# The head of a one-core encoder layer, rearranged: values before queries and keys, the norm factors applied elsewhere

## The reference, cut to what matters

```python
h = x * rsqrt(mean(x*x, axis=-1) + 1e-6) * norm_mix        # x: (512, 1024), one factor per token, one per channel
P = h @ w_in                                               # columns [q_A k_A v_A q_B k_B v_B u_C gates]
q, k = rms_norm(q_A, g_q), rms_norm(k_A, g_k)              # per head of 64
A = softmax(q k^T / 8 + bias) v_A                          # branch A; B: stick-breaking attention; C: pooling
y = (sig(g_A)*(A W_a) + sig(g_B)*(B W_b) + sig(g_C)*(C W_c)) @ W_out
x = x + y
x = x + W_down( silu(conv(hg)) * conv(hv) )                # [hg|hv] = rms_norm(x) @ W_up
```

## Time and profile before

| | us |
|---|---|
| median of 3 runs | 835.34 (834.24 to 835.59) |
| the profiled execution | 834.84 |
| its span in the trace | 832.7 |
| TensorE busy in the span | 815.1 (98%), 3855 matmuls |
| DVE, ACT, GpSimd busy | 601.5, 402.6, 102.1 |

### The profile page before, as it was taken

One profiled execution on the slowest core, in us unless ns is written; L12 is line 12 of the kernel. 1 busy time (PEld: TensorE's weight loads), 2 busy tenths in 40 slices (PEclk: granted clock), 3 DMA queues, 4 the chain that ended last, 5 costly groups with the idle time before them and its releaser, 6 DMA issues.

```text
span 832.7 us, 11778 instructions
## 1 busy us (share of the span) xinstructions
PE 815.1 (98%) x3855; PEld 677.1 (81%) x3855; DVE 601.5 (72%) x847; ACT 402.6 (48%) x560; POOL 102.1 (12%) x87
## 2 busy tenths in 40 slices
PE   5999999999999999999999999999999999899998
PEld 4888888888888888888888887888888888688886
DVE  5535888867678676555552579888778789998798
ACT  6434776665546544434341463433333334455653
POOL 2100010000000060000000013332232333300000
PEclk9999999999999999999999999999999999999999
DMA  6333242222222222333363326666556655666455
GB/s 207 103 102 89 66 124 77 79 74 66 86 76 66 74 77 88 93 98 100 89 214 104 129 72 202 203 202 201 189 191 199 196 191 185 218 210 191 149 186 177
DMA packets 129964, 113.25 MB, mean 136 GB/s; under 512 B 6052, under 2 KB 109192, under 8 KB 128528
## 3 DMA queue, kind: packets, MB, share of 16 engines
q1 hardware_dynamic: 129264, 110.77, 42.6%
q0 software_dynamic: 672, 2.12, 0.9%
HBM read 99.21 MB, written 13.65 MB: 136 GB/s over the span
## 4 chain that ended last, share of the span: by engine, by line
PE 93%; DVE 4%; ACT 1%; DMA 1%; issue 1%; SPq 0%; DVEq 0%; ACTq 0%
PE ps L1422 29%; PE ps L1423 28%; PE ps L1424 28%; PE ps L1516 2%; PE ps L1506 2%; PE ps L1531 1%; PE ps L1530 1%; DVE w_lo L872 1%; DMA x_in<-in_x_dram 1%; DVE conv_out L1259 1%; DVE out_sb L1412 0%; DVE conv_out L1262 0%; PE ps L1447 0%; DVE conv_in L1268 0%; ACT w_hi L497 0%
## 5 line engine op out<-in xcount | busy, mean ns | idle before, releaser
L1422 PE MATMUL ps<-h_lo,w_hi 128*128 128x512 f32 x704 | 276.9, 393 | 1.5 <-DVE h_lo L897 0.9
L1423 PE MATMUL ps<-h_hi,w_hi 128*128 128x512 f32 x704 | 274.2, 389 | 0.0
L1424 PE MATMUL ps<-h_hi,w_lo 128*128 128x512 f32 x704 | 274.1, 389 | 0.0
L872 DVE TENSOR_TENSOR w_lo<-w_raw,w_hi 128x1024 fp32r<-128x1024 f32 x119 | 149.8, 1259 | 137.3 <-ACT w_hi L503 77.9
L503 ACT ACTIVATE w_hi<-w_raw 128x1024 fp32r<-128x1024 f32 x97 | 102.8, 1060 | 191.9 <-PE ps L1424 183.4
L1422 PEld LDWEIGHTS ps<-h_lo,w_hi 128*128 128x128 f32 x704 | 132.2, 188 | 29.8 <-issue 1.6
L1424 PEld LDWEIGHTS ps<-h_hi,w_lo 128*128 128x128 f32 x704 | 132.2, 188 | 27.6
L1423 PEld LDWEIGHTS ps<-h_hi,w_hi 128*128 128x128 f32 x704 | 132.2, 188 | 26.5
L481 POOL TENSOR_TENSOR sg<-sg,conv_out 128x512 f32<-128x512 f32 x22 | 37.4, 1700 | 319.2 <-ACT sg L801 319.2
L1262 DVE SCALAR_TENSOR_TENSOR conv_out<-conv_in,par,conv_out 128x512 f32<-128x512 f32 x44 | 50.2, 1141 | 5.5 <-DVE conv_out L1259 0.2
L497 ACT ACTIVATE w_hi<-w_raw 128x1024 fp32r<-128x1024 f32 x23 | 24.4, 1059 | 53.3 <-PE ps L1424 53.2
(11 more groups left out here) (219 smaller groups left out, 1304.7 us busy)
## 6 DMA issues: line engine op xcount, KB each, us to landing
w_raw<-in_w_in_dram SPq DMA_DIRECT2D x104, 256.0 KB, 3.1
w_raw<-in_w_up_dram SPq DMA_DIRECT2D x88, 256.0 KB, 3.2
raw_t<-in_w_down_dram SPq DMA_DIRECT2D x11, 1024.0 KB, 9.1
down_sums<-t_sum SPq DMA_DIRECT2D x11, 1024.0 KB, 5.6
w_raw<-in_w_down_dram SPq DMA_DIRECT2D x33, 256.0 KB, 3.0
w_raw<-down_sums SPq DMA_DIRECT2D x33, 256.0 KB, 3.8
w_raw<-in_w_out_dram SPq DMA_DIRECT2D x16, 256.0 KB, 2.9
w_raw<-down_sums SPq DMA_DIRECT2D x22, 128.0 KB, 2.9
```

What stands on the lines that cost most here:

```text
L872: v.tensor_tensor(w_lo[:, slot, :], w_raw[:, slot, :], r32(w_hi[:, slot, :]), ALU.subtract)\
L1422: mm3(dst, l_hi, r_lo, start=start, stop=False, **kw)
L1423: mm3(dst, l_hi, r_hi, start=False, stop=False, **kw)
L1424: return mm3(dst, l_lo, r_hi, start=False, stop=stop, **kw)
```

## The change

The same mathematics, put differently. For the values v = diag(r) * x * diag(g) * W, with r the factor per token and g the norm weight per channel: now x itself is turned as it lands and split (`xt_hi`, `xt_lo`), g is multiplied into the weight rows when a unit of v is split (`values_hi`, `values_lo`), and r is applied when v is copied out of PSUM. So the values need no norm factors to begin. The order of units on PE becomes: v_A in units 0 to 3, the first unit of v_B (unit 4), q and k (units 5 and 6), and the rest of v_B (units 7 to 9). For q and k, and all later tiles, h is still made: the two parts of turned x are added on DVE (`h_sum`), r is spread over the partitions by two matmuls of a diagonal (`d_r_hi`, `d_r_lo`, bank `R_BANK`), and h_sum * g * r is split into `h_hi` and `h_lo`. All of that stands on ACT and DVE between the splits of the value units. The squares of x are summed later, with the first value units. At the very start PE gets 24 matmuls of 128 columns on constants, whose result is not used. The load of `g_row` moves to ACT's queue. GpSimd's one weight split is gone. `sumsq` for q and k stands after unit 7, and `newton` and `hat` behind it as before.

The diff, cut; `x_turned(t)` is two banks of PSUM, taken in turns.

```diff
-N_QK0 = 0
-N_VA = 2
+
+N_VA = 0
+N_VB0 = 4
+N_QK0 = 5
 N_VB = 6
 N_SLOT = 10
 N_MERGE = N_SLOT + 4 * 8 + 2  
...
-            def values(n0, c0):
-                for u in range(4):
-                    load(n0 + u, u % 2, [win_c[:, 2 * u + i:2 * u + i + 1, c0:c0 + WB] for i in range(2)])
-
-            cols(N_QK0, 0, win_v, Q_A)
-            cols(N_QK0 + 1, 1, win_v, K_A)
+            def values(n, u, c0):
+                load(n, u % 2, [win_c[:, 2 * u + i:2 * u + i + 1, c0:c0 + WB] for i in range(2)])
+
+            x_load(0)
+            values(N_VA, 0, V_A * P)
+            for t in range(1, TT):
+                x_load(t)
+            values(N_VA + 1, 1, V_A * P)
+            values(N_VA + 2, 2, V_A * P)
 
...
-            values(N_VA, V_A * P)
-            values(N_VB, V_B * P)
+            values(N_VA + 3, 3, V_A * P)
+            values(N_VB0, 0, V_B * P)
+            cols(N_QK0, 1, win_v, Q_A)
+            cols(N_QK0 + 1, 0, win_v, K_A)
+            for u in range(1, 4):
+                values(N_VB + u, u, V_B * P)
...
-            pool.wait_ge(hi_ready, N_QK0 + 2)
-            pool.wait_ge(lo_ready, N_QK0 + 1)
-            pool.tensor_tensor(w_lo[:, 1, :], w_raw[:, 1, :], r32(w_hi[:, 1, :]), ALU.subtract).then_inc(lo_ready, 1)
...
+            def xt_split_hi(t):
+
+                a.wait_ge(xt_done, t + 1)
+                act(xt_hi[:, :, t * P:t * P + P], x_turned(t), ACT.Copy).then_inc(xt_hi_ready, 1)
+
+            def values_hi(n, u):
+
+                a.wait_ge(w_landed[u % 2], (n // 2 + 1) * 32)
+                if n == 0:
+                    a.wait_ge(gmix_ready, 1)
+                if n >= 2:
+                    a.wait_ge(unit_done, n - 1)
+                for i in range(2):
+                    c = slice(i * WB, i * WB + WB)
+                    last = act(w_hi[:, u % 2, c], w_raw[:, u % 2, c], ACT.Copy, scale=g_mix[:, 2 * u + i:2 * u + i + 1])
+                last.then_inc(hi_ready, 1)
...
+            xt_split_hi(0)
+            values_hi(N_VA, 0)
+            for t in range(1, TT):
+                xt_split_hi(t)
+            values_hi(N_VA + 1, 1)
+            square(0)
+            square(1)
+            values_hi(N_VA + 2, 2)
+            square(2)
+            square(3)
+            a.wait_ge(ssq_done, TT)
+            act(tok[:, 2, :], tok[:, 0, :], ACT.Ln, scale=1.0 / D, bias=eps[:, :]).then_inc(ln_done, 1)
+            a.wait_ge(ln_done, 1)
+            act(tok[:, 3, :], tok[:, 2, :], ACT.Exp, scale=-0.5).then_inc(exp0_done, 1)
+            values_hi(N_VA + 3, 3)
+            values_hi(N_VB0, 0)
+            a.wait_ge(r_mix_in_psum, 1)
+            act(r_mix[:, :], ps[:, R_BANK, :], ACT.Copy).then_inc(r_mix_ready, 1)
+
+            def h_split_hi(k):
+
+                a.wait_ge(h_sum_ready, k + 2)
+                act(h_hi[:, k:k + 2, :], h_sum[:, k:k + 2, :], ACT.Copy).then_inc(h_hi_ready, 2)
+
+            h_split_hi(0)
+            h_split_hi(2)
...
-                act(h_hi[:, k, :], ps[:, k, :], ACT.Copy, scale=g_mix[:, k:k + 1]).then_inc(h_hi_ready, 1)
+                last = act(v_a[:, t, :], ps[:, V_A_BANKS[t], :], ACT.Copy, scale=tok[:, 5, t:t + 1])
+            last.then_inc(v_stored, 1)
+            h_split_hi(4)
...
-            proj_a(0, 0, 0, N_QK0 + 1, False)
-            after(N_QK0)
-            proj_a(1, 1, 1, N_QK0 + 2, False)
-            after(N_QK0 + 1)
-            after(N_VA)
-            norms_a(0)
-            after(N_VA + 1)
+            hi(N_QK0 + 1, 0)
+            proj_a(0, 0, QK0_BANK, N_QK0 + 1, False)
+            values_hi(N_VB + 1, 1)
+            proj_a(1, 1, QK0_BANK + 1, N_QK0 + 2, False)
+            values_hi(N_VB + 2, 2)
+            norms_a(0, SS0_BANK)
+            values_hi(N_VB + 3, 3)
             hat_hi(0, 0)
             hat_hi(1, 1)
...
+            def xt_split_lo(t):
+
+                d.wait_ge(xt_hi_ready, t + 1)
+                v.tensor_tensor(xt_lo[:, :, t * P:t * P + P], x_turned(t), r32(xt_hi[:, :, t * P:t * P + P]), ALU.subtract)\
+                    .then_inc(xt_lo_ready, 1)
+
+            def values_lo(n, u):
+
+                d.wait_ge(hi_ready, n + 1)
+                for i in range(2):
+                    c = slice(i * WB, i * WB + WB)
+                    last = v.scalar_tensor_tensor(out=w_lo[:, u % 2, c], in0=w_raw[:, u % 2, c],
+                                                  scalar=g_mix[:, 2 * u + i:2 * u + i + 1], in1=r32(w_hi[:, u % 2, c]),
+                                                  op0=ALU.mult, op1=ALU.subtract)
+                last.then_inc(lo_ready, 1)
+
+            def parts_added(k):
+
+                v.tensor_tensor(h_sum[:, k:k + 2, :], r32(xt_hi[:, k:k + 2, :]), r32(xt_lo[:, k:k + 2, :]), ALU.add)\
+                    .then_inc(h_sum_step, 1)
+
+            d.wait_ge(gmix_ready, 1)
+            xt_split_lo(0)
+            values_lo(N_VA, 0)
+            for t in range(1, TT):
+                xt_split_lo(t)
+            values_lo(N_VA + 1, 1)
+            d.wait_ge(xt_lo_ready, TT)
+            parts_added(0)
+            values_lo(N_VA + 2, 2)
+            parts_added(2)
...
+            d.wait_ge(tok_step, 4)
+            for t in range(TT):
+                last = v.scalar_tensor_tensor(out=d_r_lo[:, t, :], in0=ident[:, :], scalar=tok[:, 5, t:t + 1],
+                                              in1=r32(d_r_hi[:, t, :]), op0=ALU.mult, op1=ALU.subtract)
+            last.then_inc(d_r_ready, 1)
+            values_lo(N_VA + 3, 3)
+            parts_added(4)
+            parts_added(6)
...
+            d.wait_ge(r_mix_ready, 1)
+            d.wait_ge(h_sum_step, 4)
+            for k in range(KD):
+                v.scalar_tensor_tensor(out=h_sum[:, k, :], in0=h_sum[:, k, :], scalar=g_mix[:, k:k + 1], in1=r_mix[:, :],
+                                       op0=ALU.mult, op1=ALU.mult).then_inc(h_sum_ready, 1)
+            lo(N_QK0, 1)
+            for k in range(0, KD, 2):
+                d.wait_ge(h_hi_ready, k + 2)
+                v.tensor_tensor(h_lo[:, k:k + 2, :], h_sum[:, k:k + 2, :], r32(h_hi[:, k:k + 2, :]), ALU.subtract)\
+                    .then_inc(h_lo_ready, 2)
+            lo(N_QK0 + 1, 0)
+
             squares_lo(0, 0)
+            values_lo(N_VB + 1, 1)
             squares_lo(1, 1)
-            lo(N_VA + 1, 1)
-            lo(N_VA + 2, 0)
-            newton(0)
+            values_lo(N_VB + 2, 2)
+            newton(0, SS0_BANK)
             hat(0, 0)
             hat(0, 1)
-            lo(N_VA + 3, 1)
+            values_lo(N_VB + 3, 3)
             hat_lo(0, 0)
...
+            pe.wait_ge(heads_step, 2)
+            for _ in range(WARM):
+                mm3(ps[:, 2, 0:P], ones_heads[:, :], ones_heads[:, :], start=True, stop=True)
             pe.wait_ge(const_ready, 1)
...
+            def x_transposes(t):
+
+                pe.wait_ge(x_landed[t], 16)
+                if t == 1:
+                    pe.wait_ge(gmix_ready, 1)
+                if t >= 2:
+                    pe.wait_ge(xt_lo_ready, t - 1)
+                for k in range(KD):
+                    last = nc.tensor.transpose(x_turned(t)[:, k, :], x_in[:, t, k * P:k * P + P], ident[:, :])
+                last.then_inc(xt_done, 1)
...
+            for t in range(3):
+                x_transposes(t)
+            pe.wait_ge(lo_ready, N_VA + 1)
             for t in range(TT):
-                pe.wait_ge(xs_ready, t + 1)
-                for k in range(KD):
-                    last = nc.tensor.transpose(ps[:, k, t * P:t * P + P], x_scaled[:, t, k * P:k * P + P], ident[:, :])
-                    if t == TT - 1:
-                        last.then_inc(xs_used, 1)
-
-
-            tile_of(N_QK0, 0, PROJ[0], channels_ready=h_lo_ready)
-            tile_of(N_QK0 + 1, 1, PROJ[1])
+                pe.wait_ge(xt_lo_ready, t + 1)
+                for kk in range(2):
+                    last = value_product(V_A_BANKS[t], kk, t, slice(kk * WB, kk * WB + WB), 0)
+                if t == 0:
+                    x_transposes(3)
+            last.then_inc(unit_done, 1)
+            values(N_VA + 1, V_A_BANKS, 1)
+            values(N_VA + 2, V_A_BANKS, 2)
...
+            pe.wait_ge(d_r_ready, 1)
+            mm3(ps[:, R_BANK, :], ones_all[:, :], d_r_lo[:, :, :], start=True, stop=False)
+            mm3(ps[:, R_BANK, :], ones_all[:, :], d_r_hi[:, :, :], start=False, stop=True).then_inc(r_mix_in_psum, 1)
+            values(N_VA + 3, V_A_BANKS, 3)
+            pe.wait_ge(r_mix_ready, 1)
+            pe.wait_ge(par_ready, 1)
+            values(N_VB0, V_B_BANKS, 0)
+            pe.wait_ge(v_stored, 1)
+            tile_of(N_QK0, 1, QK0_BANK, channels_ready=h_lo_ready)
+            tile_of(N_QK0 + 1, 0, QK0_BANK + 1)
...
-            values(N_VA, V_A_BANKS, 0)
-            pe.wait_ge(par_ready, 1)
-            sumsq(0, 0, SS_BANK)
-            sumsq(1, 1, SS_BANK + 1)
-            for u in range(1, 4):
-                values(N_VA, V_A_BANKS, u)
-            pe.wait_ge(newton_step, 2)
-            for u in range(4):
```

(40 more changed lines are left out.)

88 lines of the change are left out of this document (50 added, 38 removed).

## The result

The changed kernel takes 840.13 us (median of 5, 839.42 to 841.09), the one before 835.59 (5 runs beside it, 834.24 to 836.17): a ratio of 1.0063, 95% interval 1.0052 to 1.0073, or 4.5 us more. The forecast was 835.0, no change, with a range of 832.8 to 838.2. The time lies outside it.

What follows compares the result with a forecast made beforehand. TensorE was taken as the bound (93% of the chain of waits). Start -4.4, spreading r +0.45 and wait +3.6 gave -0.35 us: 834.5, or 835.0 on the median's scale; range 832.8 to 838.2.

Steps and rivals of the forecast that it cites:

- the new wait: Before unit 9 on PE: its weight split, queued behind `newton` and `hat` on DVE, makes PE wait 3.6 us.
- rival 2: PE's clock falls while it stands still 3.6 us before unit 9; 2.0 us lost, 837.0 us; chance 0.12.
- The lead of the start: Kernel start: first product at 11.4 us, unit 1 at 17.9 where the second unit started at 22.29; 4.4 us gained.
- 19 slow ones and 5 fast ones: The 24 constant matmuls at PE's start: 0.21 us each while slow, then fast; 4.6 us in all, ending at 6.3.
- Rival 1: Kernel start: PE falls back to half clock for the first products; unit 1 starts 2.0 us later, 837.0; chance 0.18.
- Both rivals together: Half clock at the first products and a clock fall in the wait before unit 9: 839.0 us, chance 0.05.
- The ends of the forecast: Whole kernel: bounds from the constants' end, the stall before unit 9 and the h work, together 833.4 to 837.1 us.
- The h chain beside the values: DVE beside units 2 to 5: about 15.1 us of h work fits with about 0.5 us to spare, price 0.
- rival 4: Kernel start: late transfers shrink the gain, each us beyond 1 us of cover lost; 836 to 837 us, chance 0.07.

## Why the prediction was wrong, by its own steps

Two steps failed: the sum had no term for what PE's clock does behind the new wait, and it had the constants bring the full clock by 6.3 us.

- **The new wait** was priced at 3.6 us by starts: 69.70 less the end of unit 8's last step, 65.90 + 0.23, is 3.57. Right in cause, place and size, and shown by the split put first. One step on the way was misread without harm to the sum: before, the split behind `hat` was that of unit 5, and `sumsq` stands behind unit 2, so two units of PE work stood between them and not three, 10.9 us and not 16.3. Unit 5 started at 45.23 and its split ended at 43.22, so nobody waited, but 2.0 us were to spare and not the 7 that three units would give.
- **The wait's consequence (rival 2)** had 2.0 us and a chance of 0.12. Unit 9 took 7.17 us from its first start to the end of its last step (69.70 to 76.64 + 0.23) instead of 5.44, so 1.7. The size was nearly right; the chance was not, and the sum left the term out. "No row shows a fall after a busy stretch" was false, and so was that the trace before has no such wait to try it on: the forecast followed PE's waits through the first 80 us only, and the kernel before holds a wait of 3.96 us that ends at 728.24, with a granted clock of 0.60 and 0.55 behind it. With that row the fall is the likeliest case and the forecast is slower.
- **The lead of the start** failed too. Forecast: 4.4 us; measured: 22.29 - 20.96 = 1.33. Along the way, each counted against the forecast's own time: the constants ended at 6.9 instead of 6.3, because they ran at the low rate throughout (5.38 us, near the upper end of the bounds, 5.8); block 0 was turned and handed on 1.6 later (ACT began at 9.13, not 7.5); the first product came 1.8 later; the six products took 2.7 instead of 1.4; and unit 1 was 3.06 late. The step was "19 slow ones and 5 fast ones": I carried the rate rise at 15.0 of the kernel before over to a program that starts with other work, as if only the time spent busy counted. Rival 1 had 0.18, as a fall back to the low rate; in this profile the clock had never risen. Its price, 2.0, is two thirds of the 3.06. How much of the 3.06 is this profile's own bad luck stays open: of the four profiles with the same program up to there, unit 1 starts at 20.96 in two, at 20.50 in one and at 19.36 in one, so late in all, against 17.9.
- Both rivals together were given 839.0 and 0.05. The measured 840.1 is 1.1 more, which is what the start was later than rival 1 had it (20.96 for 19.9).
- The ends of the forecast were added up a little short: 835.0 with its low and high terms gives 833.5 and 837.4, not 833.4 and 837.1. The measured time lies outside either.
- **The rule of the Trainium skill** named with rival 1 (TensorE: Matmul & The Clock Gate, "Part 4: PE-mode transpose": the full clock does not engage for transposes) does not fit better now: after the wide constants sixteen transposes ran 0.12 us apart. The rule of the Trainium skill named with rival 2 (same page, "HAM oscillation — how this bites in real kernels": a wait between stretches throttles the array again) is borne out by the granted clock of 0.50 at 71 to 74 us and at the late wait, except that at the head the first 0.8 us behind the wait still ran at the full rate.
- **The h chain beside the values** was priced 0: PE's timeline has no idle piece from 13.22 to 65.90. Right; h_sum took 5.46 us and h_lo 4.75. DVE's splits with g took 1.41 (1.40 forecast). r's two matmuls: PE's work between 20.96 and 66.13 is 45.17 us, by the forecast 45.2.
- **The transfers** (rival 4) kept up: PE's largest idle piece between the constants and the first product, 0.90 us, was ended by `xt_lo`, a DVE split, not by a transfer.

Sum: 3.06 for the start, 1.7 for unit 9 and 0.2 before the scores make the 5.0 between 72.3 and 77.27.

What stays open: why the full clock did not come with the narrow constants, while in the kernel before it rose within transposes that are as narrow. With the same program up to there, four profiles with narrow constants have the full rate from about 15.9, 16.2, 11.6 or less, and 14.9 us on; the kernel before has it from 15.0 on, and with the late wait filled, which is the same program at the start, not before 16.0. The three profiles with wide constants have it by 7.7, 8.3 and 5.1, none of the other ten before 10.5. So that wide ones bring it early is shown by the profiles; what narrow ones do beside the scatter is not, beyond the three comparisons in which they cost or gave nothing.

## What to carry to other kernels

Before a change is priced by the engine that it relieves, follow each weight split to the unit that needs it: here one split queued behind a normalization chain, with one unit of work between instead of two, cost more than the whole reordering gained. Behind the 3.4 us wait on TensorE another 1.7 us were lost, since the clock was at half there; look for the granted clock behind the longest waits in the whole trace before pricing a new one. Matmuls without use, put into a wait that can't be removed, were worth 1.6 to 2.7 us each time here. At the start wide ones brought the full rate early, but against no constants at all what they won in time (0.07 and 0.16%) isn't clear of noise.
